# Block norms of a two-layer transformer kernel on Trainium2: last output tiles and norms computed by token halves

## The reference

```
mod = (c_act @ ada_w[i] + ada_b[i])            # sh1, sc1, g1, sh2, sc2, g2
y = diff_attention(...)  or  short_conv(a)      # layer 0, layer 1; both end in "@ w_o" / "@ w_out"
h = h + g1 * y
h = h + g2 * swiglu(rmsnorm(h, norm2[i]) * (1.0 + sc2) + sh2, ffn_w_gate_up[i], ffn_w_down[i])
rmsnorm(x, g) = x * rsqrt(mean(x * x, channels) + eps) * g
short_conv(h) = (b_gate * dwconv(c_gate * u, conv_w)) @ w_out,  b_gate, c_gate, u = split(h @ w_in)
```

## Time and profile before

| | us |
|---|---|
| median of 3 runs | 1743.03 |
| lowest, highest | 1736.89, 1743.45 |
| span of the profiled execution | 1739.3 |
| TensorE busy in the span | 1672.8 (96%) |
| VectorE busy | 975.8 (56%) |
| ScalarE busy | 677.8 (39%) |

### The profile page before, as it was taken

How to read it: one execution, slowest core, us unless ns; L and a number is a source line. 1 busy time by engine, 2 the same in 40 slices (tenths; PEclk the granted TensorE clock), 3 DMA queues, 4 the chain that set the end, 5 groups by cost and what they waited for, 6 DMA issues and landing times.

```text
span 1739.3 us, 22898 instructions
## 1 busy us (share of the span) xinstructions
PE 1672.8 (96%) x8888; PEld 1393.1 (80%) x8888; DVE 975.8 (56%) x1805; ACT 677.8 (39%) x1413; POOL 61.9 (4%) x120
## 2 busy tenths in 40 slices
PE   4999999999999999999999999999999899999999
PEld 2777777777999999777888888887888788888887
DVE  4667466766777766767555554436555533333332
ACT  3334555564455555554322222223222433333221
POOL 0000000000000000000000000000000000000000
PEclk9899998999999999998999999998999999999999
DMA  8886333313223131222666665442443233333332
GB/s 309 210 244 180 99 96 98 97 25 87 54 55 104 38 110 37 86 73 56 189 179 182 192 178 153 116 122 75 130 124 97 73 97 97 97 97 97 100 113 79
DMA packets 290215, 202.02 MB, mean 116 GB/s; under 512 B 76247, under 2 KB 272072, under 8 KB 289082
## 3 DMA queue, kind: packets, MB, share of 16 engines
q1 hardware_dynamic: 266942, 133.21, 27.5%
q0 software_dynamic: 15536, 56.37, 10.7%
q10 hardware_dynamic: 7628, 10.97, 1.9%
HBM read 197.33 MB, written 5.28 MB: 116 GB/s over the span
## 4 chain that ended last, share of the span: by engine, by line
PE 88%; DVE 6%; ACT 2%; issue 2%; DMA 2%; ACTq 1%; SPq 0%; DVEq 0%
PE PS L864 13%; PE PS L866 13%; PE PS L865 13%; PE PS L848 4%; PE PS L846 4%; PE PS L847 4%; PE PS L1285 3%; PE PS L1287 3%; PE PS L1286 3%; PE PS L1335 2%; PE PS L1094 2%; PE PS L1359 2%; PE PS L1068 2%; PE PS L1347 1%; PE PS L1076 1%
## 5 line engine op out<-in xcount | busy, mean ns | idle before, releaser
L2016 DVE TENSOR_TENSOR WL<-WS,WH 128x512 fp32r<-128x512 f32 x416 | 268.0, 686 | 256.2 <-ACT WH L1508 255.7
L1508 ACT ACTIVATE WH<-WS 128x512 fp32r<-128x512 f32 x416 | 237.7, 621 | 179.1 <-PE PS L848 130.7
L864 PE MATMUL PS<-A3H,WL 128*128 128x512 f32 x672 | 262.9, 391 | 0.1
L866 PE MATMUL PS<-A3H,WH 128*128 128x512 f32 x672 | 261.7, 389 | 0.0
L865 PE MATMUL PS<-A3L,WH 128*128 128x512 f32 x672 | 261.4, 389 | 0.0
L864 PEld LDWEIGHTS PS<-A3H,WL 128*128 128x128 f32 x672 | 126.1, 188 | 30.0 <-issue 4.4
L866 PEld LDWEIGHTS PS<-A3H,WH 128*128 128x128 f32 x672 | 126.1, 188 | 26.4
L865 PEld LDWEIGHTS PS<-A3L,WH 128*128 128x128 f32 x672 | 126.2, 188 | 26.0
L846 PE MATMUL PS<-GH,WL 128*128 128x512 f32 x352 | 137.4, 390 | 0.6 <-DVE WL L2016 0.6
L848 PE MATMUL PS<-GH,WH 128*128 128x512 f32 x352 | 137.0, 389 | 0.0
L847 PE MATMUL PS<-GL,WH 128*128 128x512 f32 x352 | 137.0, 389 | 0.0
(11 more groups left out here) (363 smaller groups left out, 3429.1 us busy)
## 6 DMA issues: line engine op xcount, KB each, us to landing
AW<-in_ada_w POOLq DMA_DIRECT2D x96, 512.0 KB, 4.1
WS<-in_ffn_w_gate_up SPq DMA_DIRECT2D x88, 512.0 KB, 4.6
WS<-in_ffn_w_down SPq DMA_DIRECT2D x32, 512.0 KB, 4.2
WS<-in_sc_w_in SPq DMA_DIRECT2D x24, 512.0 KB, 4.1
AB<-in_w_ada SPq DMA_DIRECT2D x8, 1024.0 KB, 15.7
WS<-in_w_in SPq DMA_DIRECT2D x32, 256.0 KB, 4.4
WS<-in_diff_w_qkv SPq DMA_DIRECT2D x64, 128.0 KB, 2.6
WS<-in_ffn_w_down SPq DMA_DIRECT2D x16, 384.0 KB, 3.5
```

The lines of the kernel that those rows point to most:

```text
L864: mm(PS[:, b, :], wl[:, k, :], hi[:, k, 0:S], start=(k == 0), stop=False)
L866: m = mm(PS[:, b, :], wh[:, k, :], hi[:, k, 0:S], start=False, stop=(k == KT - 1))
L1508: f(weights(p)[0][:, k, :], WS[:, p % 2, k, :], ACT.Copy).then_inc(w_hi, 1)
L2016: tt(lo[:, k, :], WS[:, p % 2, k, :], hi[:, k, :].bitcast(F32), ALU.subtract).then_inc(w_lo, 1)
```

## The change

The last output tiles ahead of the three norms (5, 6, 7 of wo2; 7 of down0; 6 and 7 of conv_out) are computed for tokens 0 to 255 first and for tokens 256 to 511 then, into another PSUM bank (HALF_BANK). Their residual, square and addition to SS are done by halves too. The sum of squares of the first half (`square_half`) is issued inside the second half's products, that of the second half inside the first pair's products (after k = 4). The three norms and the pair of panels behind them go over 8 tiles of the first token half and then 8 of the second (`norm_halves`, `linear_pair_halves`). The second half's residuals, squares and additions stand inside the first half's norm, after tile 2. The splits of the panels are moved: at the end of down0 and conv_out both first panels of the next stage are split ahead of the residuals of the halved tiles (`split_first`), and the third panel of conv_in and up1 inside the norm. ada5 is added up after the first half of tile 5, ada7a ahead of down0's last tile, ada7b and ada7c at the end of the pair's first half; ada7c thus moves behind norm_f. The gated buffer GH is cut in GA (8 tiles) and GC (14 tiles), A3H and A3L move, and the first pair of up0 gets buffers of its own (UH, UL, VH, VL). No matmul is left out; those of the halved tiles and pairs become two of 256 columns each.

```diff
...
-    ("norm_d", 1, 0, 0, 1, 0),
+    ("norm_d", 1, 0, 0, 2, 0),
...
-    ("norm_e", 1, 0, 0, 1, 0),
+    ("norm_e", 1, 0, 0, 2, 0),
...
+    ("norm_f", 1, 0, 0, 2, 0),
     ("ada7c", 1, 0, 0, 1, 0),
-    ("norm_f", 1, 0, 0, 1, 0),
...
-            return 9 + p - base
+            return (11 if base == P_UP else 9) + p - base
...
+HALF_TILES = {"wo2": (5, 6, 7), "down0": (7,), "conv_out": (6, 7)}
+HALF_OF = {"norm_d": "wo2", "norm_e": "down0", "norm_f": "conv_out"}
+HALF_BANK = {"wo2": {5: 0, 6: 5, 7: 6}, "down0": {7: 6}, "conv_out": {6: 5, 7: 6}}
+HALF_BASE = {"norm_d": 3, "norm_e": 5, "norm_f": 7}
...
+        GA = sb("GA", [P, KT, S], F32R, three)
         A3H = sb("A3H", [P, KT, S], F32R, three)
         A3L = sb("A3L", [P, KT, S], F32R, three)
-        GH = sb("GH", [P, FT, S], F32R, three)
+        with ExitStack() as first_up:
+            ABOVE = sb("ABOVE", [P, 8 * D], F32, first_up)
+            UH = sb("UH", [P, 8, P], F32R, first_up)
+            UL = sb("UL", [P, 8, P], F32R, first_up)
+            BEYOND = sb("BEYOND", [P, 6976], F32, first_up)
+            VH = sb("VH", [P, 8, P], F32R, first_up)
+            VL = sb("VL", [P, 8, P], F32R, first_up)
+        GC = sb("GC", [P, FT - KT, S], F32R, three)
...
+            def linear_pair_halves(a, hi, lo, base, between):
+                for t in range(2):
+                    take_panel(a, t)
+                tiles = [(weights(a.panel(t)), bank_of(a, t)) for t in range(2)]
+                for h in range(2):
+                    c = slice(CTX * h, CTX * (h + 1))
+                    for k in range(KT):
+                        pe.wait_ge(ln_lo, base + 8 * h + k + 1)
+                        for (wh, wl), b in tiles:
+                            mm(PS[:, b, c], wl[:, k, :], hi[:, k, c], start=(k == 0), stop=False)
+                            mm(PS[:, b, c], wh[:, k, :], lo[:, k, c], start=False, stop=False)
+                            m = mm(PS[:, b, c], wh[:, k, :], hi[:, k, c], start=False, stop=(k == KT - 1))
+                            if h and k == KT - 1:
+                                m.then_inc(w_used, 1)
+                        between(h, k)
...
+            def square_half(stage, h, beside=0):
+                a = At(stage)
+                pe.wait_ge(ss_add, squares_of(HALF_OF[stage], h) - 1)
+                wait(pe, small_free, a.small(1) if h else a.small(0) - beside)
+                c = slice(CTX * h, CTX * (h + 1))
+                mm(PS[:, SMALL, c], ONES, SS[:, c], start=True, stop=True).then_inc(small_done, 1)
...
+            for h in range(2):
+                for t in HALF_TILES["wo2"]:
+                    if h == 0 and t == 6:
+                        pe.wait_ge(x_free, len(TURNS))
+                    if h == 0 and t == 7:
+                        pe.wait_ge(wo_res, 9)
+                    if h and t < 7:
+                        pe.wait_ge(wo_res, 8 + WO2_BANK.index(HALF_BANK["wo2"][t]) + 1)
+                    elif h:
+                        pe.wait_ge(half_res, 1)
+                    out_tile(t, 1, range(4, 8), HALF_BANK["wo2"][t] if h else WO2_BANK[t], h)
+                    if h == 0 and t == 5:
+                        for x in range(2):
+                            pe.wait_ge(wo_res, 8 + WO2_BANK.index(SUM_BANKS[x]) + 1)
+                            add_beside(At("ada5"), x, 4 + x, SUM_BANKS[x])
+                    if h == 1 and t == 5:
+                        square_half("norm_d", 0, 2)
...
+                for h in range(2):
+                    for k in range(8):
+                        m = step(h, first, k, k, False)
+                m.then_inc(w_used, 1)
+                for h in range(2):
+                    for p, k0, kts in zip(others, (8, 16), (8, 6)):
+                        pe.wait_ge(w_lo, 2 * p + 2)
+                        for k in range(kts):
+                            if h == 1 and k0 == 8 and k == 5:
+                                square_half("norm_e", 0, 1)
+                            m = step(h, p, k, k0 + k, k0 == 16 and k == 5)
+                        if h == 1:
+                            m.then_inc(w_used, 1)
+                    if h == 0:
+                        m.then_inc(half_done, 1)
...
+                        def between(h, k):
+                            if h == 0 and k == 4:
+                                square_half("norm_d" if l == 0 else "norm_f", 1)
+                            if l == 1 and h == 0 and k == KT - 1:
+                                add_beside(At("ada7c"), 0, 12, SUM_BANKS[1])
+                        linear_pair_halves(a, A3H, A3L, base, between)
...
+                        if l == 0 and a.i == 3 and t == 1:
+                            add_beside(At("ada7a"), 0, 10, SUM_BANKS[1])
+                            last_down_tile(a)
+                            continue
...
+            def between_conv(h, k):
+                if h == 0 and k == 4:
+                    square_half("norm_e", 1)
+                if h == 0 and k == KT - 1:
+                    add_beside(At("ada7b"), 0, 11, 5)
...
+                for h in range(2):
+                    for t in range(2):
+                        p = a.panel(t)
+                        if h == 0:
+                            take_panel(a, t)
+                            take_acc(a, t)
+                        b = HALF_BANK["conv_out"][6 + t] if h else acc(a, t)
+                        m = linear_half(p, b, YH, YL, h, range(5))
+                        if h == 1 and t == 0:
+                            square_half("norm_f", 0)
+                        m = linear_half(p, b, YH, YL, h, range(5, KT))
+                        m.then_inc(w_used if h else half_done, 1)
...
+            def norm_halves(stage, dst, bias, between):
+                a, L = At(stage), HALF_BASE[stage]
+                root_half(a, 0)
+                for h in range(2):
+                    c = slice(CTX * h, CTX * (h + 1))
+                    for k in range(KT):
+                        act.wait_ge(ln_t, 8 * (L + h) + k + 1)
+                        f(dst[:, k, c], RAW[:, k % 2, c], ACT.Identity, bias=bias[:, k:k + 1]).then_inc(ln_hi, 1)
+                        if h == 0:
+                            between(k)
+                        if h == 0 and k == 5:
+                            root_half(a, 1)
+            def root_half(a, h):
+                c = slice(CTX * h, CTX * (h + 1))
+                act.wait_ge(small_done, a.small(h) + 1)
+                f(LT[:, c], PS[:, SMALL, c], ACT.Ln, bias=EPSC[:, 0:1], scale=1.0 / D).then_inc(small_free, 1)
+                act.wait_ge(small_free, a.small(h) + 1)
+                f(RS[:, 0, c], LT[:, c], ACT.Exp, scale=-0.5).then_inc(ln_rs, 1)
...
+            def split_first(stage):
+                if stage == "down0":
+                    split(At("down0", 3), 4)
+                    split(At("down0", 3), 5)
+                    split(At("conv_in"), 0)
+                    split(At("conv_in"), 1)
+                else:
+                    split(At("up1"), 0)
+                    split(At("up1"), 1)
...
+            def norm_halves(stage, R, hi, lo, scale, shift, gain, between):
+                L = HALF_BASE[stage]
+                stt(NS[:, :], scale, 1.0, VT[:, gain:gain + 8], ALU.add, ALU.mult).then_inc(ln_scale, 1)
+                dve.wait_ge(ln_scale, R + 1)
+                def low(h, k):
+                    c = slice(CTX * h, CTX * (h + 1))
+                    dve.wait_ge(ln_hi, 8 * (L + h) + k + 1)
+                    stt(lo[:, k, c], RAW[:, k % 2, c], shift[:, k:k + 1], hi[:, k, c].bitcast(F32),
+                        ALU.add, ALU.subtract).then_inc(ln_lo, 1)
+                for h in range(2):
+                    c = slice(CTX * h, CTX * (h + 1))
+                    dve.wait_ge(ln_rs, L + h)
+                    for k in range(KT):
+                        if k >= 2:
+                            dve.wait_ge(ln_lo, 8 * (L + h) + k - 1)
+                        stt(RAW[:, k % 2, c], H[:, k, c], NS[:, k:k + 1], RS[:, 0, c], ALU.mult, ALU.mult).then_inc(ln_t, 1)
+                        if k:
+                            low(h, k - 1)
+                        if h == 0:
+                            between(k)
+                    low(h, KT - 1)
...
-            def residual_tile(a, t, per, r, gate, more=True, squared=True):
+            def residual_tile(a, t, per, gate, more=True, squared=True):
+                if squared and a.i == 3 and t == 1:
+                    split_first(a.stage)
+                    halves(a.stage, 0, {n: acc(a, n - 6) for n in HALF_TILES[a.stage]}, gate)
+                    return
...
+            def halves(stage, h, banks, by):
+                tiles = HALF_TILES[stage]
+                for i, t in enumerate(tiles):
+                    half_residual(stage, t, h, banks[t], by)
+                    if i:
+                        add_half(stage, tiles[i - 1], h)
+                add_half(stage, tiles[-1], h)
...
-            for t in range(8):
```

(52 more changed lines are left out.)

208 lines of the change are left out of this document (141 added, 67 removed).

## The result

The changed kernel takes **1755.08 us** (median of 5 runs, 1753.02 to 1758.68) against 1741.95 for the kernel before (5 runs): a ratio of **1.0082**, 95% interval 1.0071 to 1.0093. The forecast of 1751 was 4 us too low; the range held the time, but its likeliest class was "within 0.5%" (0.46 against 0.42 for slower), and the kernel is slower by more than that.

A forecast was written before the change was run, and what follows sets the result against it. The prediction took TensorE, busy 96%, as the bound, with VectorE bounding pairs by halves. Chains of 4.9 us plus 3.2 for the clock gave +8.1 on the 1739.3 span; with 3.7 carried over, 1751 us, range 1739 to 1759.

The forecast's parts named there:

- within 0.5%: Outcome class for the whole kernel: a time not told from no change, 0.5% being 8.7 us; chance 0.46.
- VectorE's price: Pairs by halves: VectorE's half tile takes 0.92 us against TensorE's 0.72, making each pair 3.0 us longer.
- the waits: TensorE idle 2.7 us at norm_d's tile 2, 1.6 at tile 6, 2.9 and 3.1 at down0's and conv_out's column sums.
- the insertion at tile 2: Second half's residuals and additions in VectorE's first-half norm: 2.6 us at norm_d, 1.3 at norm_e, 1.9 at norm_f.
- the second root at tile 6: First half's norm: second column sum, logarithm and exponential stand ahead of tile 6, making its remainder 1.6 us late.
- the walk: Step-by-step sum at full clock to each pair's end: +0.8 us at norm_d, +2.0 at norm_e, +2.1 at norm_f.
- A: The forecast case for the whole kernel: 1747 to 1755 us, also given as 1746 to 1756; chance 0.45.
- the clock: Half clock behind new waits and one-column work: between 0 and 14 us, taken as two places, 3.2 us.
- the six places: Feared half clock: three idle stretches of 2.7 to 3.1 us, ada5, and waits before one-column work at norm_e and norm_f.
- rival B: Slower: half clock follows each new stall, five or six places at 1.6 to 2.3 us, 1758 us; chance 0.28.
- C: Faster: TensorE kept fed in the pairs if half tiles take 0.72 us or less, 1727 to 1734 us; chance 0.12.
- D: Nothing: earlier pair start and longer norm cancel, clock no worse, 1738 to 1748, say 1745 us; chance 0.15.

The follow-up runs named there:

- e9: e6 with VectorE's scalings in the three norms over 64 instead of 256 columns, part of the norm left out: 1734.84 us, ratio 0.9963.
- e3: The changed kernel with the second first-panel split (conv_in's and up1's panel 1) behind the first halves' residuals and squares: 1745.2 us, ratio 1.0029.
- e6: e5 with ScalarE's second logarithm and exponential behind tile 6 of the first half instead of tile 5: 1740.82 us, ratio 1.0003.
- e2: The changed kernel with ada7b and ada7c behind the pair's second half instead of between its halves: 1753.81 us, ratio 1.0071.
- e1: The changed kernel with ada5 behind tile 7's first half instead of tile 5's, the column sum right behind it: 1751.81 us, ratio 1.0059.
- e12: e6 with ada7b and ada7c again between the pair's halves and the third panel's split behind the norm: 1738.45 us, ratio 0.9979.
- e4: The changed kernel with VectorE's scalings in the three norms over 64 instead of 256 columns, part of the norm left out: 1751.56 us, ratio 1.0061.
- e5: The changed kernel with the three moves of e1, e2 and e3 together: 1743.79 us, ratio 1.0016.
- e10: e6 with the third panel's split (conv_in's and up1's) behind the norm instead of inside its first half: 1740.36 us, ratio 0.9989.

## Why the prediction was right and wrong

**Right, VectorE's price.** "The pair by halves is bound by VectorE: 16 x 0.915": the pace is 0.92 in the trace, and e9 shows it as the bound. The fp32 formula of the Trainium skill (VectorE: DVE Perf Modes, The TRN2 errata) made an estimate of 0.85 for it; the trace does not agree, the row of norm_b was the better source. A scaling of 64 columns took 0.28 (e9).

**Right, the waits.** All four, within 0.5 us, with their causes: the insertion at tile 2, the second root at tile 6, the load and split that now stand ahead of the residuals. In e3, with the split moved, the waits in down0 and conv_out are gone; in e6, with the root moved, the wait at tile 6 is gone, though two thirds of it come back at the next two tiles of norm_d. The insertion at tile 2 was not tested by itself. The waits were foreseen; that the split's place was a free choice, and the costliest one, was not said.

**Right, the walk.** +0.8, +2.0, +2.1 at full clock. norm_f in e2, at 1.00 throughout, takes 33.7 us without the bare sum behind it: +2.0. At norm_e the kernel after comes to its first scaling 19.5 us from the start (the walk has 19.1), and e3 goes on from there in 20.0 (20.0): together +2.4. norm_d in e1, with ada5 moved, is at +0.4; in its own order it was never seen at full clock. Slips in the recorded sums (the first half of tile 7 adds up to 794.0, not 794.1; 3.4/2 is 1.7, not 1.6; A's range is given twice, as 1747 to 1755 and 1746 to 1756) change nothing.

**Wrong, one term: the clock, "I take two, 3.2 us".** Five of the six places slowed, and 10.7 us lie beyond the walk, 2.1 a place on average (1.3 to 2.9), where the prediction had a price of 1.6 to 2.3 for one. The step that failed is the reason for taking two: "part of the slow matmuls lie where VectorE bounds anyway". Of the five only the stretch at 806.57 is of that kind, and even it cost 1.3; behind ada5 and behind down0's column sum TensorE was the bound, and the 16 records of ada7b took 3.27 us instead of 1.85, more than VectorE's backlog covers. That was rival B, at 0.28 the second likeliest, with its time of 1758 for five or six places: B's mechanism is what happened, 3 us short of its time, and it deserved the larger chance, since the condition it named (about three places) was met by the waits that the walk itself had found.

**Right by luck, part of the time.** The span was forecast as 1747.4 and is 1755.6, 8.2 off. The time is only 4 off, because 3.7 us were carried over from span to median where the runs show 1.8 between a run's span and its time, and the profiled execution is 2.3 above the median of the changed kernel.

**Rivals C and D** fell. C's condition was a half tile at 0.72 us, and it is 0.92. e9 has that pace, at the price of a part of the norm, and comes to 6.4 us under the kernel before, not 15.7; the best whole kernel, e12, to 3.7. D had the early start and the longer norm cancel at 1745; the walk alone, which the measured parts bear out, is +4.9 (1748), and half clock came on top.

**Not settled.** Why the clock fell at down0's column sum after 2.67 us of waiting and not at conv_out's after 2.73. e1, e2 and e4 have both waits again, from 2.67 to 2.88 us, with the same work ahead: at down0's the clock fell in all four profiles (in e1 1.2 us behind the sum), at conv_out's in two of four (e1 and e4). So the second place slows in one execution and not in another; what decides it stays open.

## What to carry to other kernels

Halving a norm to start the next product early pays little where the slower engine's time for a half tile stays above TensorE's; here two VectorE operations cost 0.92 for TensorE's 0.72, which took 7.0 us, and the best order of the rest left 3.7 us of gain. Where a list is reordered for such an overlap, look for what the old order had hidden in a wait (a split behind the residuals, one-column sums in the gap of the norm): moved into a busy stretch, each costs its own time and may slow what stands behind it. When a walk finds new waits and low-activity work on TensorE, price half clock at every one of them that stands ahead of work that could run at once. The mean clock of the run does not show this loss: it was 0.979 in both kernels, and only the place of the slow stretches differed.

## What the runs showed of the hardware

One-column fp32 sums count as busy in the profile (794.09 to 803.67 is 5.65 us of busy TensorE at clock 0.68). Still, in all fourteen profiles (before, after, e1 to e12) the clock fell to 1.2 GHz during ada5's 3.7 us of them or within 1.2 us behind. ada7a, 1.85 us of the same work between full products, was followed by no fall in any of the twelve profiles in which it stands ahead of down0's last tile. Pairs with waits of 0.5 to 1.2 us and no sums between their halves kept 2.4 GHz in nine of ten places (norm_e and norm_f of e2, e5, e6, e9, e10; norm_f of e5 did not), pairs with a sum there in four of twelve. This leans one way and is no rule.

Whether a given place slows is not fixed by the program: conv_out's column sum slowed in two of four profiles, and identical runs of e3 spread over 14 us with the mean clock. The Trainium skill (TensorE: Matmul & The Clock Gate, Part 1) says that the chip's view of activity is not started anew by a kernel, so that a transition falls at another place from run to run; these two observations agree with it.
